# Value tiles of a two-block sequence mixer: weights as the stationary operand, then a turn to token order

## The reference

```python
h = h + HALF * _swiglu(_rmsnorm(h, ffn1_norm[l]), ffn1_w_in[l], ffn1_w_out[l])
xn = _rmsnorm(h, mix_norm[l])
z = xn @ w_in[l]
z_rw = z_rw + shift_mu[l] * (_time_shift(z_rw) - z_rw)
y_a = _rwkv7_mixer(r, k, v, xw, xa, xg, ...)
y_b = _mlstm_mixer(mq, mk, mv, mo, mi, mf, ...)   # q, k: causal conv of 4 taps, then silu
u = sigmoid(g_a) * (y_a @ br_a[l]) + sigmoid(g_b) * (y_b @ br_b[l])
h = h + u @ w_out[l]
h = h + HALF * _swiglu(_rmsnorm(h, ffn2_norm[l]), ffn2_w_in[l], ffn2_w_out[l])
```

## Time and profile before

| | |
|---|---|
| median of 3 runs | 2619.52 us (2617.49 to 2622.0) |
| the profiled execution | 2617.78 us |
| its span, first to last instruction | 2615.8 us |
| mean granted TensorE clock | 0.962 of full |
| PE busy | 2434.9 us, 93% |
| DVE, ACT, POOL busy | 48%, 38%, 9% |
| DMA | mean 148 GB/s |

### The profile page before, as it was taken

How to read it: one execution, slowest core, us unless ns; L and a number is a source line. 1 busy time by engine, 2 the same in 40 slices (tenths; PEclk the granted TensorE clock), 3 DMA queues, 4 the chain that set the end, 5 groups by cost and what they waited for, 6 DMA issues and landing times.

```text
span 2615.8 us, 50326 instructions
## 1 busy us (share of the span) xinstructions
PE 2434.9 (93%) x20748; PEld 2207.6 (84%) x20748; DVE 1248.7 (48%) x1990; ACT 1002.4 (38%) x1594; POOL 224.7 (9%) x199
## 2 busy tenths in 40 slices
PE   7999799899989799999999799999999987989998
PEld 3754599799966599989998688899999977888998
DVE  1152355555424255465567353455555565443554
ACT  3153433354334353343345331334433454321433
POOL 0000000000000000010005231100100033321000
PEclk9999899989989999989999799999999998999999
DMA  6154354354424545345533112544445231114552
GB/s 256 70 176 174 144 190 172 128 183 178 160 81 166 189 169 191 146 164 186 184 112 108 55 67 106 212 181 180 164 174 191 105 129 65 66 67 161 201 184 96
DMA packets 64486, 388.05 MB, mean 148 GB/s; under 512 B 7152, under 2 KB 7280, under 8 KB 27376
## 3 DMA queue, kind: packets, MB, share of 16 engines
q1 hardware_dynamic: 63216, 379.61, 39.8%
q10 hardware_dynamic: 864, 5.16, 0.5%
q0 software_dynamic: 288, 1.57, 0.2%
HBM read 385.27 MB, written 1.05 MB: 148 GB/s over the span
## 4 chain that ended last, share of the span: by engine, by line
PE 79%; DVE 5%; issue 5%; POOL 4%; ACT 4%; DMA 2%; POOLq 0%; SPq 0%; DVEq 0%; ACTq 0%
PE ps L1707 19%; PE ps L1708 19%; PE ps L1709 19%; PE ps L1783 5%; POOL t_lo L555 3%; PE ps L1796 2%; PE ps L2221 2%; PE ps L2068 2%; DMA ring_a<-in_wa 2%; POOL h_lo L533 1%; PE ps L2259 1%; PE ps L1677 1%; PE ps L2194 1%; PE ps L1654 1%; PE ps L1811 1%
## 5 line engine op out<-in xcount | busy, mean ns | idle before, releaser
L1707 PE MATMUL ps<-h_hi,w_hi 128*128 128x256 f32 x2464 | 702.6, 285 | 12.4 <-DVE mod L1063 8.7
L1708 PE MATMUL ps<-h_lo,w_hi 128*128 128x256 f32 x2464 | 700.5, 284 | 0.0
L1709 PE MATMUL ps<-h_hi,w_lo 128*128 128x256 f32 x2464 | 700.5, 284 | 0.0
L1707 PEld LDWEIGHTS ps<-h_hi,w_hi 128*128 128x128 f32 x2464 | 476.6, 193 | 14.7 <-DVE mod L1063 9.6
L1708 PEld LDWEIGHTS ps<-h_lo,w_hi 128*128 128x128 f32 x2464 | 476.5, 193 | 0.1
L1709 PEld LDWEIGHTS ps<-h_hi,w_lo 128*128 128x128 f32 x2464 | 476.3, 193 | 0.0
L1125 DVE TENSOR_TENSOR w_lo<-ring_a,w_hi 128x1024 fp32r<-128x1024 f32 x308 | 366.4, 1231 | 30.0 <-ACT w_hi L634 29.8
L1708 PE MATMUL ps<-hid_lo,d_hi 128*128 128x256 f32 x1232 | 348.7, 283 | 0.0
L1707 PE MATMUL ps<-hid_hi,d_hi 128*128 128x256 f32 x1232 | 348.7, 283 | 0.0
L1709 PE MATMUL ps<-hid_hi,d_lo 128*128 128x256 f32 x1232 | 348.6, 283 | 0.0
L634 ACT CAST w_hi<-ring_a 128x1024 fp32r<-128x1024 f32 x308 | 306.0, 1044 | 61.9 <-DMA ring_a<-in_wa 61.9
(11 more groups left out here) (282 smaller groups left out, 3296.9 us busy)
## 6 DMA issues: line engine op xcount, KB each, us to landing
ring_a<-in_wa SPq DMA_DIRECT2D x278, 1024.0 KB, 4.8
ring_d<-in_wd SPq DMA_DIRECT2D x154, 512.0 KB, 5.3
work<-in_wa SPq DMA_DIRECT2D x6, 1024.0 KB, 21.7
work<-in_small POOLq DMA_DIRECT2D x2, 768.0 KB, 5.6
c<-in_c ACTq DMA_DIRECT2D x1, 1175.0 KB, 10.4
work<-in_c ACTq DMA_DIRECT2D x1, 1088.0 KB, 5.0
x<-in_x ACTq DMA_DIRECT2D x1, 1024.0 KB, 14.8
work<-in_ctx ACTq DMA_DIRECT2D x1, 1024.0 KB, 19.3
```

What stands on the lines that cost most here:

```text
L1707: nc.tensor.matmul(out, hi, to_hi, start=start, stop=False, skip_group_check=True)
L1708: nc.tensor.matmul(out, hi, to_lo, start=False, stop=False, skip_group_check=True)
L1709: return nc.tensor.matmul(out, lo, to_hi, start=False, stop=stop, skip_group_check=True)
```

## The change

The value tiles become ordinary tiles. `value_tiles` and `empty_values` go. Tiles 27 to 30 are made by `tile` (24 matmuls each, weights stationary), ACT copies each into a small buffer (`vraw`, the memory that later holds the exponentials `ems`), eight transposes on PE turn all four to token order in banks 6 and 7, and ACT copies those two banks to `mv`. The Silu of q and k moves ahead of the emptying of tile 30. In the second layer alone the head norms are made behind tile 23 instead of ahead of tile 22, and what stood between tiles 22 and 28 comes two tiles later. Head 0 waits for the new `mv` step.

```diff
-        ems = [v[:, i, :] for v in (sg, hid) for i in range(2)]
+        ems = vraw = [v[:, i, :] for v in (sg, hid) for i in range(2)]
-        MA = Steps(["ab", "ex", "ln", "silu", "hq", "hsd", "so"])
-        MP = Steps(["if", "mu", "var"])
+        MA = Steps(["ab", "ex", "ln", "silu", "mv", "hq", "hsd", "so"])
+        MP = Steps(["if", "mvt", "mu", "var"])
-                def empty_values(t):
-                    act.wait_ge(t_done, l * NT2 + t + 2)
-                    both = ps[:, 5 if t == MV else 4, :].rearrange("p (b s n) -> p s b n", b=2, s=2)
-                    for u in range(2):
-                        j = t + u - MV
-                        nc.scalar.copy(mv[:, :, j * P:(j + 1) * P], both[:, (t + u) % 2]).then_inc(t_free, 1)
-                    round_t(t + 2)
-                    round_t(t + 3)
+                def empty_value(t):
+                    act.wait_ge(t_done, l * NT2 + t + 1)
+                    nc.scalar.copy(vraw[t - MV], ps[:, 4 + t % 2, 0:T]).then_inc(t_free, 1)
+                    round_t(t + 2)
...
+                later = 2 * l
+                empties(23, 23 + later)
                 to_tokens(v_t, 6).then_inc(rw_a, 1)
-                empty_t(24)
+                empties(24 + later, 24 + later)
                 to_tokens(khc_t, 6).then_inc(rw_a, 1)
-                empty_t(25)
-                empty_t(26)
+                empties(25 + later, 26 + later)
                 to_tokens(bhc_t, 0).then_inc(rw_a, 1)
-                empty_values(MV)
+                empties(27 + later, 28)
...
-                empty_values(MV + 2)
+                empties(29, 29)
                 nc.scalar.activation(nsq[:, :, :], nsq[:, :, :], ACT.Silu).then_inc(ml_a, 1)
+                empties(30, 30)
+                act.wait_ge(ml_p, MP.at("mvt", l))
+                for b in range(2):
+                    ins = nc.scalar.copy(mv[:, b, :], ps[:, 6 + b, :])
+                ins.then_inc(ml_a, 1)
...
+                if l == 0:
+                    head_norms()
                 tile(22)
+                if l:
+                    tile(23)
+                    head_norms()
                 pe.wait_ge(rw_a, RA.at("gg", l))
+                pe.wait_ge(rw_v, RV.at("rkr", l))
                 to_tokens(z[:, V0:V0 + QT, 1:T + 1], 6).then_inc(rw_p, 1)
-                tile(23)
+                if l == 0:
+                    tile(23)
+                else:
+                    tile(24)
+                    tile(25)
                 per_unit(0, bh, kt).then_inc(rw_p, 1)
                 per_unit(2, kt, bh).then_inc(rw_p, 1)
-                tile(24)
+                n = 24 + 2 * l
+                tile(n)
                 to_tokens(khc, 6).then_inc(rw_p, 1)
                 per_unit(0, kh, rt).then_inc(rw_p, 1)
-                tile(25)
+                tile(n + 1)
                 per_unit(2, bh, rt).then_inc(rw_p, 1)
                 per_unit(6, kh, kt).then_inc(rw_p, 1)
-                tile(26)
+                tile(n + 2)
                 to_tokens(bhc, 0).then_inc(rw_p, 1)
-                value_tiles(MV)
+                for t in range(n + 3, MV + 2):
+                    tile(t)
...
-                value_tiles(MV + 2)
+                tile(29)
+                tile(30)
+                pe.wait_ge(t_free, p0 + GATES)
+                pe.wait_ge(rw_v, RV.at("mt", l))
+                for b in range(2):
+                    for j in range(QT):
+                        mm = nc.tensor.transpose(ps[:, 6 + b, j * P:(j + 1) * P], vraw[j][:, b * P:(b + 1) * P], ident)
+                mm.then_inc(ml_p, 1)
...
+                    if h == 0:
+                        pe.wait_ge(ml_a, MA.at("mv", l))
```

More of the change, by code:

```diff
@@ L954, in to_tokens, with empties @@
                     return ins
-                empty_t(23)
+                def empties(first, last):
+                    for t in range(first, last + 1):
+                        (empty_t if t < MV else empty_value)(t)
+                later = 2 * l
+                empties(23, 23 + later)
                 act.wait_ge(rw_p, RP.at("vt", l))
@@ L1975, in tile @@
                     mm.then_inc(t_done, 1)
[L1977 to L1990, removed]
                 for t in range(4):
@@ L2034, in _, with head_norms @@
                     tile(t)
[L2035 to L2047, removed]
+                def head_norms():
+                    pe.wait_ge(rw_v, RV.at("rn", l))
+                    if l:
+                        pe.wait_ge(vres_a, 1)
+                    hr = const("headrow")
+                    for j in range(QT):
+                        mm = nc.tensor.matmul(ps[:, j // 2, half(j)], hr[0:8, cols(j)], inv_norm, start=True, stop=True)
+                    mm.then_inc(rw_p, 1)
+                    pe.wait_ge(rw_v, RV.at("rkr", l))
+                    for j in range(QT):
+                        mm = nc.tensor.matmul(ps[:, 2 + j // 2, half(j)], const("headones"), bon[:, j, :],
+                                              start=True, stop=True)
+                    mm.then_inc(rw_p, 1)
+                if l == 0:
+                    head_norms()
                 tile(22)
@@ L2162, in _ @@
                 mm.then_inc(ml_p, 1)
-                pe.wait_ge(ml_a, MA.at("hsd", l))
                 for i in range(len(LEVELS)):
```

## The result

The changed kernel takes 2590.86 us (median of four runs, 2588.45 to 2593.11) where the kernel before took 2619.42 us (median of four) on the same chip: a ratio of 0.989, 95% interval 0.9873 to 0.9907. The predicted time was 2593.5. The profiled execution took 2591.31 us, with a span of 2589.4.

The account below looks back on a forecast made before the run. PE, busy 93% of the span, was taken as the bound, with gain only where it stands still. The heads' starts, 12.7 + 13.3 = 26.0 us earlier, gave 2591.8 for the profiled execution, 2593.5 for the median; range 2586 to 2602.

Parts of the forecast that it names:

- The waits and the order: First layer, value tiles to heads' start: single tiles without the pair waits start the heads at 1458.8, 12.7 us earlier.
- The taps: DVE's 24 taps ahead of Silu: each POOL half among them adds about 1.0 us, 17.9 us in the first layer.
- taps that aren't lengthened: Rival, chance 0.08: POOL's halves don't lengthen the taps enough to matter, heads 15.1 and 16.4 us earlier, 2588.
- The second layer: Second layer, tile 22 to heads' start: with the norms behind tile 23, the heads start 13.3 us earlier.
- The term that was short: DVE's row chain behind the taps: takes 4.3 us and is just hidden by the transposes.
- norms' move: Second layer's head norms behind tile 23: worth little, 13.3 us against about 12.7 with the first layer's order.
- The sum: Both layers' heads' starts: 12.7 + 13.3 = 26.0 us less, 2593.5 for the median.
- the rest moves as a block: Everything behind the heads' start: all engines find the same order, so it only moves earlier.
- The rival of the kept clock: Rival, chance 0.06: the heads' first stretch keeps its clock, some 6 us a layer less, 2581.5.
- The slower rival: Rival, chance 0.02: clock stays low behind the heads' start, up to 2.95 us more per gate tile; 2629 at twelve.
- The wait for POOL that stays: Rival, chance 0.04: each single value tile still waits for POOL, only half of 9.2 us a layer won, 2610.
- The second layer's bound: Rival, chance 0.07: DVE and POOL become the second layer's bound, last masked copy 6.6 us later still, 2600.

Follow-up runs that it names:

- pool_waits_nm: The changed kernel with POOL's remainders of tiles 31 and later held until the row chain is done; 2586.70 us.
- filler: The changed kernel with PE multiplying useless tiles (34 in the first layer, 48 in the second) while it waits for tile 30's emptying; 2590.91 us, second time 2586.06.
- the run of the token tiles: The changed kernel with each value tile made alone, activations stationary, straight into token order, without transposes or their copies; 2591.92 us.
- silu_behind: The changed kernel with the Silu put back behind the emptying of tile 30; 2594.89 us.

## Why the prediction was right

**The waits and the order.** Each step of the first layer fell where it was put: tiles 27 to 30 end at 1451.94 (said: 1451.95), the taps at 1454.56 (1454.3), Silu at 1456.50 (1456.3), the transposes at 1458.79 (1458.8).

**The taps.** They were said to be lengthened by POOL's halves at 1.0 us each, to 17.9 us (six halves more than before) and 13.9; measured 18.03 and 13.96, with eight and four halves beside them in all. pool_waits_nm shows the cause by taking two away. Of the rivals this one, taps that aren't lengthened (2588), is out.

**The second layer.** Counted in the time of the kernel before (plus 11.1), the norms start at 2150.7 (said: 2150.7) and take 1.99 twice, PE stands 3.25 us ahead of tile 24 (about 3), the taps run 2185.0 to 2199.0 (2184.8 to 2198.7). DVE and POOL are in each other's way there as forecast, without becoming the bound: PE's only other wait for POOL there is 0.46 at tile 25.

**The term that was short.** "The row chain ... just hidden by the transposes": it wasn't, by 0.46 us in each layer. The 4.3 us were taken over from the kernel before, where a half lengthens the chain's second operation by 0.7 us. In the changed kernel that one is short again, and the half meets the last one. First layer, before and after:

```profile
1456.89 1.11 DVE L1471 TENSOR_TENSOR work<-work 4x256 f32<-4x256 f32 x1
...
1454.98 0.41 DVE L1476 TENSOR_TENSOR work<-work 4x256 f32<-4x256 f32 x1
```

So the chain takes 4.7 us, and it starts 0.3 us later than said. In the second layer the prediction's own terms left less room than it gave: 2198.7 + 4.3 is 2203.0 and not 2202.5.

The Trainium skill ("SBUF — State Buffer", section "Who interferes with whom") says that a `tensor_scalar`, too, can enter a mode that takes the port pair shared with GpSimd, when its operands meet that mode's conditions, and that whoever issues first holds the pair for the whole instruction. The trace agrees: 1.38 us behind a half begun 0.02 us before, 0.28 us in pool_waits_nm. With this, and 0.1 us of transposes in the second layer, 12.7 and 13.3 become the 12.4 and 12.7 measured, within 0.2.

**What the norms' move is worth.** I gave it 0.6 us of the second layer (13.3 against 12.7 with the first layer's order). By the heads' start it is 2.0 us, so its price was too low by 1.4; by the time it is nothing that can be measured. The step was small in the sum and stays unsettled between these.

**The sum.** The heads' starts give 12.4 + 12.7 = 25.1 us, 0.9 less than the 26.0 of the prediction. The spans differ by 26.4. The other 1.3 is a balance of stretches that the change doesn't touch: 1.1 and 1.5 less from the heads to the branch product, 2.2 more between the two layers' parts, 1.1 less at the end and 0.1 more at the start. Each of them is smaller than the 3.0 us by which the time behind one wait varies with the clock. It is luck that they bring the spans closer to 26.0 than the heads' starts are. The medians differ by 28.6 us; the 2.2 beyond the spans stand in no trace, and the four executions of the changed kernel lie up to 4.7 apart. "Behind the heads' start all engines find the same order, so the rest moves as a block" holds to that accuracy; the first gate tile behind the heads, for one, came out 0.8 us longer in the first layer and 1.3 in the second. (The chances given to the faster cases add up to 0.97, not 0.96.)

**The rival of the kept clock** (2581.5) did not occur: the stretch behind the heads' start is at the low level after the change as before it. Windows of the changed kernel, from the heads' first product and over the first gate tile:

```profile
1459.00:1471.00 12.00, 11.75 (x31) 9.20 (x32) 1.87 (x4) 4.13 (x7) 1.32 (x2) 0.50 0.00 0
1471.00:1477.00 6.00, 6.00 (x33) 5.92 (x32) 0.56 (x1) 0.95 (x3) 0.00 (x0) 0.63 0.00 0
...
1477.00:1500.00 23.00, 22.58 (x158) 20.99 (x157) 14.15 (x20) 9.20 (x13) 11.09 (x9) 1.00 0.27 92
```

Part of its gain can be had: filler reaches 2.3 and 2.5 us of it by the heads' first mask, though its total shows nothing clear of the scatter. The slower rival (a clock that stays low in the gate tiles) is refuted by the last of these windows, which begins ahead of the second gate tile (1479.6) and stands at 1.00. The wait for POOL that stays (2610) is refuted by PE's waits, which have none for POOL at the value tiles. The second layer's bound (2600) is refuted by its taps, which start where they were put.

## What to carry to other kernels

Where one engine waits for work that arrives in pairs, making the items one by one can win the whole wait; here the form in which they are made changed nothing in the total. Then lay every instruction of the engine that lengthens the path's operations against each of them, the tiny last one too: here each half of POOL cost the path about one us (eight in the first layer's taps, one in a row operation). Holding POOL back, moving the row chain between the taps and taking Silu off the way to the heads' first product won another 14 us together; of this the runs give 4.2 to POOL alone and don't split the rest. To compare edits of a few us, measure from marks around the edit and look at the clock of each of PE's waits, because the total scatters by more than the edit.

## What the runs showed of the hardware

- The clock of PE after the same short wait is not the same from one execution to the next. The 3.2 us ahead of the branch product left a clock of 1.00, over the eight us around it, in the first layer of one execution and 0.59 in that of another. The 13 profiles hold 26 such waits: 1.00 six times, 0.79 nine times, 0.57 or 0.59 eleven times. The second product then comes 3.8 us behind the wait's end, or 5.2 to 5.4, or 6.5 to 6.8. What decides it isn't shown here.
- The clock also falls while PE is shown busy. In the run of the token tiles the heads' first products ran at 2.4 GHz and the small products five us behind them at 1.2, with no wait of PE between. In the filler runs the same products took 1.99 us once and 3.31 once. In the first layer of silu_behind and of the second filler run the clock was 0.79 over 1410 to 1418, where the changed kernel had 1.00; PE is shown busy for all of the 8.00 us in each of them, and the taps started 1.65 us later. The changed kernel first, then silu_behind:

```profile
1410.00:1418.00 8.00, 8.00 (x62) 7.79 (x62) 7.91 (x6) 5.94 (x7) 3.80 (x3) 1.00 0.41 148
1410.00:1418.00 8.00, 8.00 (x46) 7.03 (x45) 7.54 (x6) 5.62 (x8) 2.51 (x2) 0.79 0.50 174
```

- One half of POOL lengthens DVE's run of 128x255 operations with two SBUF inputs by 1.0 us, as forecast (18.03 against 15.99 us for two halves), and an operation of 4x256 with one input by 1.1 us (1.38 against 0.28).
